# Exchanging the operands of the modulation products and spreading them over six stages of a two-layer diffusion backbone

## The reference

```python
s_c = silu(c); s_ctx = silu(c_ctx)
for layer in range(2):
    mod  = split(s_c   @ ada_w[layer] + ada_b[layer], 6)   # latent tokens; ada_w is 1024 x 6144
    modc = split(s_ctx @ ada_w[layer] + ada_b[layer], 6)   # context tokens
    h = rms_norm(x, norm1_g[layer]) * (1 + mod[1]) + mod[0]
    # ... mixers ...
    x = x + mod[2] * (y @ w_out)
    h = rms_norm(x, norm2_g[layer]) * (1 + mod[4]) + mod[3]
    x = x + mod[5] * peer(h)
```

## Time and profile before

| | us |
|---|---|
| median of 3 runs | 6425.05 (6415.15 to 6425.99) |
| the profiled execution, own time | 6423.28 |
| its span | 6421.4 |
| TensorE busy | 1980.0 (31%) |
| VectorE busy | 4624.4 (72%) |
| GpSimd busy | 2779.1 (43%) |
| ScalarE busy | 707.9 (11%) |

### The profile page before, as it was taken

One profiled execution on the slowest core, in us unless ns is written; L12 is line 12 of the kernel. 1 busy time (PEld: TensorE's weight loads), 2 busy tenths in 40 slices (PEclk: granted clock), 3 DMA queues, 4 the chain that ended last, 5 costly groups with the idle time before them and its releaser, 6 DMA issues. The chain is left out here.

```text
span 6421.4 us, 34050 instructions
## 1 busy us (share of the span) xinstructions
PE 1980.0 (31%) x9185; PEld 1340.5 (21%) x9185; DVE 4624.4 (72%) x7420; ACT 707.9 (11%) x984; POOL 2779.1 (43%) x2800
## 2 busy tenths in 40 slices
PE   8798687760000000000000047867770000000001
PEld 2485486550000000000000032633360000000000
DVE  0114574238898998989989842589328899898898
ACT  0212421210000000000000022444220000000000
POOL 0100031106566675666767620045104567566665
PEclk9897898885555555555555578977885555555555
DMA  7310001118899999999999920000126899899997
GB/s 253 112 56 2 4 4 27 46 66 336 303 346 369 338 392 338 354 348 336 407 340 401 374 95 15 8 5 0 46 79 246 303 334 404 318 366 359 378 364 307
DMA packets 452648, 1473.60 MB, mean 229 GB/s; under 512 B 55126, under 2 KB 91724, under 8 KB 449900
## 3 DMA queue, kind: packets, MB, share of 16 engines
q0 software_dynamic: 368640, 1342.34, 55.2%
q1 hardware_dynamic: 83536, 129.04, 6.0%
q10 hardware_dynamic: 284, 0.09, 0.0%
HBM read 1458.72 MB, written 12.58 MB: 229 GB/s over the span
## 5 line engine op out<-in xcount | busy, mean ns | idle before, releaser
L1311 POOL DMA_INDIRECT rows<-peer_u,expert x1280 | 1223.4, 956 | 1285.6 <-DVE expert L1458 487.4
L1507 DVE CUSTOM_DVE_ANT_0 junk<-rows,banks 128x1024 f32<-128x1024 f32 x1280 | 1493.8, 1215 | 212.8 <-DVE dots L1507 92.3
L1513 DVE SCALAR_TENSOR_TENSOR banks<-rows,weight,banks 128x1024 f32<-128x1024 f32 x1260 | 1530.9, 1283 | 30.0 <-DVE banks L1513 1.6
L1311 POOL DMA_INDIRECT rows<-peer_v,expert x1280 | 1208.1, 944 | 488.7 <-issue 320.0
L1332 PE MATMUL banks<-ident,y_tok 128*128 128x128 f32 x80 | 19.7, 427 | 3324.7 <-DVE y_tok L1476 1912.3
L1332 PEld LDWEIGHTS banks<-ident,y_tok 128*128 128x128 f32 x80 | 15.7, 223 | 3327.4 <-DVE y_tok L1476 1913.8
L2000 POOL TENSOR_TENSOR prods<-s,cos 128x512 f32<-128x512 f32 x64 | 81.0, 1265 | 589.6 <-DVEq L1986 589.6
L359 POOL TENSOR_TENSOR h_lo<-sq,h_hi 128x768 fp32r<-128x768 f32 (+1 forms) x32 | 68.1, 2164 | 520.1 <-ACT h_hi L351 520.1
L939 POOL TENSOR_TENSOR z<-expo,keep_k 128x384 f32<-128x384 f32 x28 | 30.8, 1105 | 557.1 <-ACT expo L915 557.1
L1325 PE MATMUL banks<-ident_r,h_hi 128*128 128x128 f32 x80 | 33.6, 420 | 559.7 <-DVEq L1529 546.4
L1358 ACT COPY y_tok<-banks 128x1024 f32<-128x1024 f32 x10 | 10.1, 1012 | 1616.2 <-issue 1267.2
(11 more groups left out here) (340 smaller groups left out, 5628.5 us busy)
## 6 DMA issues: line engine op xcount, KB each, us to landing
ada_ring<-ada_w SPq DMA_DIRECT2D x24, 2048.0 KB, 8.0
rows<-peer_u,expert POOLq DMA_INDIRECT x1280
rows<-peer_v,expert POOLq DMA_INDIRECT x1280
peer_wq_in<-peer_wq SPq DMA_DIRECT2D x16, 1024.0 KB, 5.6
y_t<-ev_w_in SPq DMA_DIRECT2D x12, 1024.0 KB, 5.4
scores<-score_out SPq DMA_DIRECT2D x10, 1024.0 KB, 3.9
score<-scores SPq DMA_DIRECT2D x10, 1024.0 KB
od_in_in<-od_w_in SPq DMA_DIRECT2D x4, 1024.0 KB, 5.4
```

The lines of the kernel that those rows point to most:

```text
L1311: pool.indirect_dma_start(out=ring[:, at % RING, :], out_offset=None, in_=tables[kind == "v"], in_offset=bass.IndirectOffsetOnAxis(ap=expe ...
L1507: last = nc.vector.tensor_tensor_reduce(out=junk[:, s % 2], in0=row, in1=tile_h(t), scale=1.0, scalar=0.0, op0=ALU.mult, op1=ALU.add, accu ...
L1513: last = nc.vector.scalar_tensor_tensor(out=acc(s % 2), in0=row, scalar=weight[:, t, s:s + 1], in1=acc(s % 2), op0=ALU.mult, op1=ALU.add)
```

## The change

`stage_modulation` is gone. A class `ModPiece` computes two parts of a layer (16 tiles of 128 channels) in eight pieces of 256 columns, 1 MB each. In it the weights are the stationary operand, a 128x128 block at a time, and `cond` streams past with its two columns, so results come out by channels and neither rows nor turns are needed. `keep` adds the bias for all 16 tiles in one VectorE instruction and computes `gs` where a scale part is among them.

| stage | parts | buffer, slots of 1 MB | where on TensorE |
|---|---|---|---|
| load_tokens | layer 0: 0, 1 | own, 8, loaded on ScalarE's queue | after the last token tile |
| norm, layer 0 | layer 0: 2, 3 | in `hg`, 6 | after the sums of squares |
| gqa_heads | layer 0: 4, 5 | own, 3 | four pieces ahead of the first tile, one ahead of each of tiles 2 to 5 |
| hgrn2_gates | layer 1: 0, 1 | own, 3 | alone |
| norm, layer 1 | layer 1: 2, 3 | own, 3 | after the sums of squares |
| s5_parameters | layer 1: 4, 5 | own, 3 | after the first transpose, ahead of the 32 jobs |

The loads of the five later stages go on SP's queue; in the norm stages the first ones stand ahead of the two weight blocks. In `stage_load_tokens` the small vectors are now turned after the first tile. `stage_gqa_heads` uses three PSUM slots in place of four. Products end up in PSUM bank 7 (bank 0 in the gates).

```diff
+MOD_COLS = 2 * P
+class ModPiece:
+    def __init__(self, a, g, layer, first, last, ring, at):
+        self.g, self.layer, self.first, self.n, self.ring, self.at = g, layer, first, last - first, ring, at
+        self.slots = min(ring.shape[1], self.n)
...
+    def load(self, engine, j):
+        if j >= self.slots:
+            engine.wait_ge(self.summed, j - self.slots + 1)
+        c = (self.first + j) * MOD_COLS
+        engine.dma_start(self.ring[:, j % self.slots], self.src[:, :, c:c + MOD_COLS])\
+            .then_inc(self.loaded[j % self.slots], 16)
+
+    def products(self, nc, pe, j):
+        pe.wait_ge(self.loaded[j % self.slots], 16 * (j // self.slots + 1))
+        for m in range(2):
+            at = self.at + (2 * j + m) * 2
+            for k in range(DK):
+                last = nc.tensor.matmul(self.g.ps[:, at:at + 2], self.ring[:, j % self.slots, k, m * P:(m + 1) * P],
+                                        self.g.cond[:, k], start=(k == 0), stop=(k == DK - 1))
+        last.then_inc(self.summed, 1)
+
+    def keep(self, nc, dve):
+        g, layer, tiles, m0 = self.g, self.layer, 2 * self.n, 2 * self.first
+        own = Steps(dve, self.scaled)
+        dve.wait_ge(self.summed, self.n)
+        own(nc.vector.tensor_tensor(
+            g.mod[:, layer, m0:m0 + tiles, :], g.ps[:, self.at:self.at + 2 * tiles].rearrange("p (m s) -> p m s", s=2),
+            g.ada_b[:, 48 * layer + m0:48 * layer + m0 + tiles].unsqueeze(2).to_broadcast([P, tiles, 2]), ALU.add))
+        own.settle()
+        for which, (norm, part) in enumerate((("norm1", 1), ("norm2", 4))):
+            if not m0 <= 8 * part < m0 + tiles:
+                continue
...
 def stage_load_tokens(nc, g):
...
+            pe.wait_ge(const_loaded, 16)
+            turn_tokens(0)
             pe.wait_ge(rows_loaded, n_rows)
...
+            for j in range(1, T // P):
+                turn_tokens(j)
+            pe.wait_ge(cond_ready, 1)
+            for j in range(8):
+                mod.products(nc, pe, j)
...
+            for j in range(8):
+                mod.load(act, j)
             for j in range(T // P):
                 act.wait_ge(transposed, j + 1)
...
+                if j == 0:
+                    act.wait_ge(vec_ready, 1)
+                    nc.scalar.activation(g.cond[:], g.vec[:, 0:16].rearrange("p (s k) -> p k s", s=2), ACT.Silu)\
+                        .then_inc(cond_ready, 1)
-def stage_modulation(nc, g):
...
 def stage_norm(...)
+            for j in range(mod.slots if mod else 0):
+                mod.load(sp, j)
             for b, (c0, cols, _) in enumerate(blocks[:W_RING]):
                 sp.dma_start(weight_slots(room)[:, b, :, 0:cols], w_view[:, :, c0:c0 + cols]).then_inc(w_loaded, 16)
+            for j in range(mod.slots, mod.n) if mod else ():
+                mod.load(sp, j)
...
             last.then_inc(summed, 1)
+            for j in range(mod.n if mod else 0):
+                mod.products(nc, pe, j)
...
 def stage_gqa_heads(...)
+            for j in range(mod.n - NT + 2):
+                mod.products(nc, pe, j)
             for t in range(NT):
+                if t >= 2:
+                    mod.products(nc, pe, mod.n - NT + t)
                 pe.wait_ge(ready, t + 1)
...
 def stage_s5_parameters(...)
             nc.tensor.transpose(ps[:, 0:3 * N], rows[:], g.ident[:3 * N, :3 * N]).then_inc(turned, 1)
+            for j in range(mod.n):
+                mod.products(nc, pe, j)
             for n in range(len(jobs)):
                 pe.wait_ge(pad_ready, n + 1)
```

More of the change, by code:

```diff
@@ L109, in block @@
         return self.stack.enter_context(self.nc.Block())
+MOD_COLS = 2 * P
[3 more added lines that the diff above has]
+        self.slots = min(ring.shape[1], self.n)
+        self.loaded = [a.sem(f"mod_loaded{r}") for r in range(self.slots)]
+        self.summed, self.scaled = a.sem("mod_summed", "mod_scaled")
+        self.src = g.d["ada_w"][layer].rearrange("(k p) n -> p k n", p=P)
+    def load(self, engine, j):
[23 more added lines that the diff above has]
+                continue
+            at = VEC[norm][0] + 8 * layer
+            gs = g.gs[:, layer, which]
+            own(nc.vector.tensor_scalar(gs, g.mod[:, layer, 8 * part:8 * part + 8, :], 1.0, None, ALU.add))
+            own.settle()
+            own(nc.vector.tensor_tensor(gs, gs, g.vec[:, at:at + 8].unsqueeze(2).to_broadcast([P, 8, 2]), ALU.mult))
+            own.settle()
@@ L112, in stage_load_tokens, with mod_ring @@
+def mod_ring(flat, slots):
+    return flat[:, 0:slots * DK * MOD_COLS].rearrange("p (r k c) -> p r k c", r=slots, k=DK)
 def stage_load_tokens(nc, g):
@@ L136, in _, with turn_tokens @@
         def _(pe):
-            pe.wait_ge(const_loaded, 16)
-            for j in range(T // P):
+            def turn_tokens(j):
                 pe.wait_ge(tile_loaded, 16 * (j + 1))
@@ L301, with stage_norm @@
+                if j == 0:
+                    act.wait_ge(vec_ready, 1)
+                    nc.scalar.activation(g.cond[:], g.vec[:, 0:16].rearrange("p (s k) -> p k s", s=2), ACT.Silu)\
+                        .then_inc(cond_ready, 1)
 STREAMS = ((1, 0, CTX), (0, CTX, T))
-def stage_norm(nc, g, layer, which, t0, hi, lo, room, w_view, blocks, latents_first=False):
+def stage_norm(nc, g, layer, which, t0, hi, lo, room, w_view, blocks, latents_first=False, later=None):
     n = T - t0
@@ L328, in stage_norm @@
         own_v = a.sem("own_v")
+        mod = later and ModPiece(a, g, *later, 7 * BANK)
         block = a.block()
@@ L386, in _ @@
                                                    op0=ALU.mult, op1=ALU.mult).then_inc(scaled, 1)
+            if mod:
+                mod.keep(nc, dve)
 W_RING, W_COLS = 2, 256
@@ L515, in token_units, with stage_gqa_heads @@
     return [("tokens", j, out[:, j, :]) for j in range(tiles)]
-def stage_gqa_heads(nc, g, proj, q_t, k_t):
+def stage_gqa_heads(nc, g, proj, q_t, k_t, later):
     NT, NH, N = T // P, GQA_Q + GQA_KV, (GQA_Q + GQA_KV) * HEAD
@@ L770, in build @@
         g.x_t = a.sb("x_t", [P, DK, T])
+        g.cond = a.sb("cond", [P, DK, 2])
         stage_load_tokens(nc, g)
-        stage_modulation(nc, g)
         if until >= 1:
@@ L780, with stage_hgrn2_gates @@
 NL = len(HG_LEVELS) + 1
-def stage_hgrn2_gates(nc, g, hg, forget, keep_k, cum):
+def stage_hgrn2_gates(nc, g, hg, forget, keep_k, cum, later):
     N = HG_HEADS * T
@@ L797, in stage_hgrn2_gates, with _ @@
         logits = g.vec[:, at:at + 16].rearrange("p (d e h) -> p d e h", d=2, e=2)
+        @block.sync
+        def _(sp):
+            for j in range(mod.n):
+                mod.load(sp, j)
+        @block.tensor
+        def _(pe):
+            for j in range(mod.n):
+                mod.products(nc, pe, j)
         @block.scalar
@@ L1674, with stage_s5_parameters @@
 ROUND = 1.5 * 2.0 ** 23
-def stage_s5_parameters(nc, g, rate, turns, b_t, c_t):
+def stage_s5_parameters(nc, g, rate, turns, b_t, c_t, later):
     N = 2 * S5_TILES
@@ L1697, in stage_s5_parameters @@
             "pad_kept")
+        mod = ModPiece(a, g, *later, a.sb("ada_ring", [P, 3, DK, MOD_COLS]), 7 * BANK)
         block = a.block()
@@ L2135, in layer_even @@
                     k_t = c.sb("k_t", [P, T])
-                    stage_gqa_heads(nc, g, proj, q_t, k_t)
+                    stage_gqa_heads(nc, g, proj, q_t, k_t, (0, 16, 24))
                 if until >= 3:
@@ L2192, in layer_odd @@
                     room = e.sb("od_in_in", [P, W_RING * DK * W_COLS])
-                    stage_norm(nc, g, 1, 0, 0, hi, lo, room, w_in, blocks)
+                    with ExitStack() as ring_scope:
+                        ring = Arena(nc, ring_scope).sb("ada_ring", [P, 3, DK, MOD_COLS])
+                        stage_norm(nc, g, 1, 0, 0, hi, lo, room, w_in, blocks, later=(1, 8, 16, ring))
                     stage_project_split(nc, g, "od_in", hi, lo, w_in, blocks, room)
@@ L2218, in layer_odd @@
                 z_t = y_t[:, 4:DK]
-                stage_s5_parameters(nc, g, rate, turns, b_t, c_t)
+                stage_s5_parameters(nc, g, rate, turns, b_t, c_t, (1, 16, 24))
                 stage_s5_scan(nc, g, u_t, rate, turns, b_t, c_t, z_t)
```

29 lines of the change are left out of this document (19 added, 10 removed).

## The result

| | before | after |
|---|---|---|
| median of 7 runs, us | 6417.86 (6411.56 to 6428.12) | 6436.23 (6428.01 to 6442.69) |
| the profiled execution, own time | 6423.28 | 6428.01 |
| its span | 6421.4 | 6426.2 |
| TensorE busy | 1980.0 | 2096.9 |

What follows compares the result with a forecast made beforehand. Stage by stage, TensorE paced the 204.0 us modulation stage; its low-clock loads would price the new places. Token stage -139.0, norms +48.4, GQA +37, gates +30.9, S5 +48.5 made +25.8 on 6423.3: 6449 us, range 6290 to 6468.

Steps and rivals of the forecast that it cites:

- the price of a place: In each of six places, 256 load-and-multiply pairs on TensorE at the low clock, with waits at eight pieces: 56.7 us.
- 6 C - 314.4: Whole change in us, C being the products' time in a place, if TensorE ends every place last; zero at C = 52.4.
- The modulation stage gone, norm starting at 91.3: Token stage takes the first products; norm of layer 0 starts at 91.3 instead of 230.26 us: -139.0 us.
- the bound of 36: Token stage: first product expected at 33 us, with bounds of 30 and 36.
- 0.218 us a pair at the lower clock: TensorE, all six places: each load-and-multiply pair takes 0.218 us at 1.2 GHz, against 0.111 at 2.4.
- The 214 ns worked out for the load: TensorE: loading 128 columns costs 214 ns at 1.2 GHz, from maxima of 127 (two columns) and 338 ns (128 columns).
- the 4 ns added for the rest of the pair: TensorE: the few ns a full-speed pair has above its load, taking 214 ns to 0.218 us.
- the 0.1 us for the wait at each piece: Each place: about 0.1 us of waiting at each of eight pieces, taking 55.9 us to 56.7.
- Granted clock 0.50 in every place: TensorE runs the products at 1.2 GHz in all six places, since they stream two columns per 128 loaded.
- Norms, +24.2 each: Norm stages of layers 0 and 1: products after the sums of squares outlast GpSimd, +24.2 us each, together +48.4.
- GQA heads +37, gates +30.9, S5 +48.5: Three later stages: products outlast their cover, lengthening GQA heads by 37 us, HGRN2 gates by 30.9, S5 parameters by 48.5.
- The full clock's rival: All six places: products granted 2.4 GHz after some 4 us, 31.2 us a place; sum -130.5, 6293 us; chance 0.25.

Runs made afterwards that it cites:

- the issues spread: ScalarE issues two first loads at the start, then one per evacuated tile: changed kernel, ratio 1.0026; version streaming 128 columns with the S5 part moved, 6001.8 us.
- 128 columns: Changed kernel with cond's two columns streamed 64 times over in each product: 6274.59 us, ratio 0.981 to the kernel before.
- hiding without exchange: Changed kernel's six places, but cond loaded and weights streamed as before, the turn to channels left out: 6051.55 us, ratio 0.9834 to the kernel before.
- both moves: S5's parts moved to layer 0's second norm stage: changed kernel, 6145.33 us, ratio 0.9988; version streaming 128 columns, 6006.52 us, ratio 0.9761.
- 64 columns: Changed kernel with cond's two columns streamed 32 times over in each product, one run: 6376.28 us, 22.8 under the kernel before.
- 32: Changed kernel with 32 moving columns in place of two, one run: 6422.73 us, 23.7 over the kernel before.
- the kernel without hiding: Changed kernel's operands, but the ten later parts in five stages of their own behind the token stage: 6569.49 us, ratio 1.0266 to the kernel before.

## Why the prediction came out as it did

The direction, the clock and each stage's new end were as forecast; the size was not: +25.8 us were summed, +15.7 came. The mechanism was right. The step that failed is the size of one term, the price of a place, which was taken as 56.7 us (256 pairs at 0.218 and 0.8 for waits between pieces). It measured 54.2 to 54.8, and 50 to 52 where the clock was still up from the sums of squares; the six together some 320 us, where the sum has 333 (six times 56.7 less 3.5 for each norm). By the prediction's own formula, 6 C - 314.4 with its zero at C = 52.4, a result of +25.8 rests on 4.3 us between price and zero, and 2 to 2.5 of those were not there. Later first products (3.7 us in the token stage, 1.1 in S5) took part of this back, and 10.1 us are left. The sum was a small difference of large terms.

- *The modulation stage gone, norm starting at 91.3.* 92.14. Two errors cancel: the first product came at 36.74, beyond the bound of 36 for the forecast 33; the products were 2.5 us shorter. ScalarE was held until 27.6, as forecast, but that is worth only 2.4 us of the delay: with the issues spread the first product still came at 34.34, as each tile of tokens was awaited from its transfer.
- *0.218 us a pair at the lower clock.* 0.2139 (54.77 / 256), 2% less. The 214 ns worked out for the load from two maxima of the earlier trace rows were the pair's whole price; that the maxima gave it so exactly is partly luck, as with the median of 333 ns in place of 338 the same working gives 209. What was too much are the 4 ns added for the rest of the pair and the 0.1 us for the wait at each piece: the rows show a wait before the first piece of a place only.
- *Granted clock 0.50 in every place.* So it was, but for the start of three: 2.6 and 4.7 us at full clock in the norms, behind the sums of squares, and half a microsecond in the token stage, behind the last tile's turns.
- *Norms, +24.2 each.* +23.9 and +20.4. Their products took 52.18 and 50.27 us, 2.6 and 4.5 less than a whole place at the lower level; 3.5 had been counted for each.
- *GQA heads +37, gates +30.9, S5 +48.5.* +34.2, +28.0, +47.3, with their first pieces 7.3, 5.2 and 16.5 us into the stage (forecast 7.4, 5.8, 15.4): each is shorter by about the shorter place, S5 less so, as its first piece was later. The first padded turn in S5 came at 4160.08, 71.1 us into its stage; before it came after 23: 48 us late, as forecast.
- *The full clock's rival* was wrong for this kernel, and its prices were right: with 128 columns the token stage came out 162 us shorter (it said 164.5), GQA heads +7.3 (9.8), gates +3.8 (5.4), S5 +21.9 (22.8), the sum -131.6 (-130.5). The rule it came from (the Trainium skill, "TensorE: Matmul & The Clock Gate", Part 1), that activity releases the gate, holds in this trace only for some activity: TensorE without a gap for 54 us stayed at 0.50.
- The Trainium skill, same page, LDWEIGHTS, has a load at columns / 1.2 GHz, without the array's clock in it. The traces disagree: the pairs that load the same 128 columns take 0.2139 us at the lower level and 0.1123 (28.75 / 256) at the upper.

What is shown: the lower clock is the cause of the loss (128 columns), exchange and hiding have opposite signs (168 us lost by the one without most of the other, 108 won by hiding without exchange), and the S5 place was the dearest (both moves). Not shown is why two streamed columns leave the clock low while 128 raise it; the runs give the states, not the rule behind them.

## What to carry to other kernels

A product that loads a full block of weights to stream two columns is paid by its load, and in this kernel it also took TensorE's clock down to half, where 1536 pairs cost some 320 us instead of 173. Before exchanging operands, ask what the granted clock will be; if it falls, streaming the same few columns many times over may bring it back at no cost: here 128 columns did, 64 kept it only where it was up already, and 32 did not. When work is moved under other work, add up the place's own cover: a norm stage in which GpSimd ends 30 us after TensorE's last sum took the work for nothing at full clock, and a stage whose chain waits on the same TensorE queue paid for nearly all of it.

## What the runs showed of the hardware that was not expected

- The clock can stay in either state for a whole place: with 64 columns, 54.7 us at the slow pace in the token stage, and 28.7 at the fast one in the norm stage behind it.
- The clock column is not enough by itself near the start of a run. In the 64-column kernel it reads 1.00 for a stretch in which the pairs go at the slow pace, 49 in 10 us, and in the kernel without hiding it does the same; the durations decide:

```profile
50.00:60.00 10.00, 10.00 (x49) 10.00 (x48) 0.00 (x0) 0.00 (x0) 0.00 (x0) 1.00 0.00 0
```

- Issuing is not free on a compute engine: eight 1 MB loads held ScalarE for 22.28 us, though the first two took 1.08 us when they were issued alone.
- Changing between the two kinds of product costs: a piece of 16 passes and four pairs took 4.09 us where the parts were expected to add up to 3.86. Of this, 0.16 us lie at the two changes: from the last pass to the next pair 0.309 us instead of the 0.216 between passes, and back 0.181 instead of the 0.112 between pairs.
